# Query projections of a cross attention and five gate panels in seven block products

## The chip, the cores and the metric

One core of a Trainium2 chip runs the whole program. The time is that of one execution on the device in microseconds (us). Everything is computed in fp32.

## The reference

Two transformer blocks follow each other on 256 rows of width 1024. The parts that the change touches, with their shapes:

```
# first block: token mixer, once
proj  = h @ w_in                       # [256, 1024] @ [1024, 7880]
gates = proj[:, 4808:]                 # 3 x 1024 columns: a, b, c
score = sum_h w_idx[h] * relu(q_idx[h] @ k_idx.T / 8) / sqrt(8)   # 8 index heads
keys  = the 64 largest scores of each row                         # for attention c
y = sigmoid(gates_a) * (o_a @ w_branch_a) + sigmoid(gates_b) * (o_b @ w_branch_b)
  + sigmoid(gates_c) * (o_c @ w_branch_c)

# second block: cross attention on a memory of 256 rows, in each of 2 layers
q    = (x @ wq).reshape(256, 4, 256)   # wq [1024, 1024]
k, v = split(memn @ wkv)
x    = layer_norm(alpha * x + softmax(q @ k.T / 16) @ v @ wo)
```

## The kernel before

TensorE (PE) multiplies, VectorE (DVE) adds, combines and normalizes, ScalarE (ACT) copies results out of PSUM and computes exponentials and sigmoids, GpSimd (POOL) makes one sum per panel and clears paddings, and SyncE (SP) issues the loads of the weights. Each engine has its order written out by hand, in one block of the program each; semaphores that only count upwards tie them together. There is no scheduler.

**Panels.** The weights pass as panels of 1024 x 512 values (2 MB) through a ring of four slots. SP issues the load of panel n when panel n - 4 has counted up `panel_done`. `P_WIN + j` are the panels of the first block's input projection: nine whole ones, one of 200 columns, then six gate panels, of which the sixth (the late gate) is multiplied in eight pieces between the units of the first attention. `L_WQ`, `L_WQ + 1` are the two panels of the query projection in a layer.

**Seven products.** The two feed-forward networks, the nine whole panels of the first input projection and three of each layer's split activations and weight panel into 2 x 2 blocks and form the result from seven products of blocks in place of eight. That costs sums. DVE makes three sums of weight quarters per panel (`weight_sums`, lines 1886 to 1890, each 128 x 1024 values; it counts up `forms_ready`), the fourth sum is POOL's (`fourth_sums`, line 610, `fourth_ready`) or DVE's own (line 1893). `act_sums` (lines 1902 to 1907) makes the sums of the turned activations once, when both tiles have been turned. ACT copies the first product out of its bank (`first_out`), and DVE combines the rest in three to four additions (lines 1934 to 1941 where rows of the result lie on the partitions, 2400 to 2412 where its columns do). `project` (product on line 822) works in rows and `expand_turned` (line 878) in columns. Both start with the first tile: turn it, products 1 and 2 of panel 0 (a head), turn the second tile, head of panel 1, then products 6, 7, 5, 4, 3 (a tail) of each. Product 6 waits for `forms_ready`, product 4 for `fourth_ready`.

**Eight products.** The gate panels (`gate` on PE, line 1127) are multiplied plainly, 16 matmuls with 512 columns each, in two halves, one for each tile of 128 rows; ACT's sigmoid reads the banks directly (line 1540). Between the halves PE turns the heads of the three attentions (`batch`, line 977, in banks 4 and 5) and computes index scores (`index_scores`, line 1160). ACT applies the relu to them (line 1555), DVE adds them up with their weights (line 2188) and, after four of them, takes the 64 largest of a tile in eight rounds of eight (lines 2202, 2204). The query projection of a layer (`weight_stationary`, line 716) is 32 matmuls with 256 columns per panel; ACT copies and scales the result (line 1671). Ahead of it PE multiplies half of the memory's values (`memory_values(1, ...)`, line 1351, copied out by ACT on line 1694) and turns both tiles of the normalized rows (batches `E_X1`).

**The first attention** (`attend`) runs 20 units. In step j PE computes the scores of unit j, turns the weights of unit j - 2 and multiplies values of unit j - 3; DVE makes the logits (line 2030) and, in the first eight units, mixes two maps (line 2057). The last four units need the selected keys.

## Time and profile before

| what | us |
|---|---|
| median of 3 runs | 1814.26 |
| lowest, highest | 1813.68, 1817.46 |
| the profiled execution, whole | 1820.03 |
| its span from first to last instruction | 1818.2 |
| PE busy in it | 1751.6 |
| DVE busy | 1058.7 |
| ACT busy | 360.0 |
| POOL busy | 191.0 |
| mean granted clock of TensorE | 0.99 of 2.4 GHz |

All durations used below are of the profiled execution. A line of a timeline merges neighbouring records of one form: its start, the time from its start to its end, and the idle time of the engine before it with what ended that. The starts of neighbouring lines give the pace; the ends of matmuls are modelled and reach a little over the next start.

### The profile page before, as it was taken

Reading aid. Unit: us, or ns where it says so; the run is one execution under the profiler, and the core shown is the slowest. Engines: PE = TensorE matmul, PEld = TensorE weight load, DVE = VectorE, ACT = ScalarE, POOL = GpSimd, SP = SyncE. Lnnn points to the kernel's source line nnn. Section 1 sums busy time; section 2 is a strip of 40 time slices with the busy share of each in tenths; the row PEclk is TensorE's granted clock in tenths of the full one; section 3 lists DMA queues with packets and bytes.
Section 4 is the critical chain, followed back from the end, with each engine's and each line's share of the span. In section 5 each row is a group of like instructions: output and inputs, shape, how many; then the busy total and the mean of one; then the engine's idle time right before and its main releaser. Section 6 shows DMA issues by size and latency. Waiting matters only on the chain.

```text
span 1818.2 us, 22081 instructions
## 1 busy us (share of the span) xinstructions
PE 1751.6 (96%) x8510; PEld 1293.5 (71%) x8510; DVE 1058.7 (58%) x2084; ACT 360.0 (20%) x884; POOL 191.0 (11%) x126
## 2 busy tenths in 40 slices
PE   6999999999999999999999999999999999999997
PEld 5887478744747885476784859984668766689953
DVE  5776468724654786641172158995712541479985
ACT  1111000033411110102271212220012530222210
POOL 1221211100011122120001000002110000000020
PEclk9999999999899999999999999999999999999999
DMA  9643454531166454436314335443455205165440
GB/s 313 207 154 142 159 185 157 185 116 70 55 209 202 148 183 162 147 105 192 139 45 142 124 116 180 150 180 131 143 145 190 88 1 208 47 209 167 159 162 23
DMA packets 162502, 265.59 MB, mean 146 GB/s; under 512 B 4008, under 2 KB 105684, under 8 KB 162270
## 3 DMA queue, kind: packets, MB, share of 16 engines
q1 hardware_dynamic: 157470, 248.18, 40.2%
q0 software_dynamic: 4768, 15.48, 2.5%
q8 instruction: 68, 1.11, 0.3%
q10 hardware_dynamic: 160, 0.52, 0.1%
q14 instruction: 36, 0.29, 0.1%
HBM read 262.56 MB, written 1.08 MB: 145 GB/s over the span
## 4 chain that ended last, share of the span: by engine, by line
PE 76%; DVE 14%; DVEq 4%; ACT 3%; issue 2%; DMA 1%; SPq 1%; ACTq 0%
PE psum L766 15%; PE psum L926 11%; PE psum L822 10%; PE psum L739 8%; PE psum L1044 4%; PE psum L1127 3%; PE psum L1079 3%; PE psum L1308 3%; PE psum L1351 3%; PE psum L716 3%; DVE work L2379 3%; PE psum L977 2%; DVE ring L1888 2%; PE psum L729 2%; PE psum L965 2%
## 5 line engine op out<-in xcount | busy, mean ns | idle before, releaser
L610 POOL TENSOR_TENSOR work<-ring,work 128x1024 f32<-128x1024 f32 (+1 forms) x57 | 141.5, 2483 | 808.9 <-DVE work L1890 808.9
L926 PE MATMUL psum<-ring,work 128*128 128x512 f32 x352 | 162.2, 596 | 3.5 <-DVE work L2412 3.5
L1886 DVE TENSOR_TENSOR work<-ring 128x1024 f32<-128x1024 f32 (+1 forms) x83 | 100.8, 1214 | 84.9 <-PE psum L926 80.8
L739 PE MATMUL psum<-ring,x_t 128*128 128x512 f32 x320 | 140.0, 595 | 7.4 <-ACT x_t L1408 7.4
L926 PEld LDWEIGHTS psum<-ring,work 128*128 128x128 f32 x352 | 66.5, 190 | 85.3 <-issue 80.1
L926 PE MATMUL psum<-work 128*128 128x512 f32 x264 | 123.1, 595 | 0.0
L739 PEld LDWEIGHTS psum<-ring,x_t 128*128 128x128 f32 x320 | 60.0, 190 | 81.5 <-issue 71.8
L1888 DVE TENSOR_TENSOR ring<-ring 128x1024 f32<-128x1024 f32 (+1 forms) x83 | 102.3, 1233 | 6.2
L1890 DVE TENSOR_TENSOR work<-ring 128x1024 f32<-128x1024 f32 (+1 forms) x83 | 99.6, 1200 | 6.2
L926 PEld LDWEIGHTS psum<-work 128*128 128x128 f32 x264 | 50.1, 192 | 62.9 <-issue 61.2
L2030 DVE CUSTOM_DVE_ANT_0 work<-psum,work 128x256 f32<-128x256 f32 (+1 forms) x96 | 31.4, 365 | 108.8 <-PE psum L1044 108.7
L1044 PE MATMUL psum<-work 128*128 128x256 f32 (+2 forms) x416 | 85.3, 337 | 3.4 <-ACT work L1671 2.2
L766 PE MATMUL psum<-ring,x_t 128*128 128x256 f32 x352 | 83.2, 391 | 3.7 <-ACT x_t L1408 2.2
L878 PE MATMUL psum<-x_t,work 128*128 128x128 f32 x704 | 85.8, 275 | 0.0
L878 PE MATMUL psum<-work,ring 128*128 128x128 f32 x704 | 85.8, 275 | 0.0
L2379 DVE SCALAR_TENSOR_TENSOR work<-work 128x254 f32<-128x254 f32 (+1 forms) x176 | 83.5, 527 | 3.3
L878 PE MATMUL psum<-x_t,ring 128*128 128x128 f32 x704 | 82.6, 276 | 2.8 <-ACT x_t L1408 2.8
L1408 ACT ACTIVATE work<-psum 128x512 f32<-128x512 f32 (+4 forms) x84 | 44.9, 562 | 194.5 <-PE psum L977 163.0
L766 PE MATMUL psum<-work,x_t 128*128 128x256 f32 x352 | 83.2, 379 | 0.0
L766 PE MATMUL psum<-ring,work 128*128 128x256 f32 x352 | 83.2, 379 | 0.0
L878 PEld LDWEIGHTS psum<-x_t,ring 128*128 128x128 f32 x704 | 80.4, 192 | 3.8 <-ACT x_t L1408 3.8
L878 PEld LDWEIGHTS psum<-x_t,work 128*128 128x128 f32 x704 | 82.1, 192 | 0.0
(258 smaller groups left out, 2919.9 us busy)
## 6 DMA issues: line engine op xcount, KB each, us to landing
ring<-in_ffn_w_up_dram SPq DMA_DIRECT2D x66, 1024.0 KB, 7.9
ring<-in_w_in_dram SPq DMA_DIRECT2D x21, 2048.0 KB, 7.8
ring<-in_ffn_w_down_dram SPq DMA_DIRECT2D x20, 2048.0 KB, 7.7
ring<-in_ffn_w_gate_dram SPq DMA_DIRECT2D x22, 1024.0 KB, 5.4
ring<-in_xa_wkv_dram SPq DMA_DIRECT2D x8, 2048.0 KB, 7.9
ring<-in_w_out_dram SPq DMA_DIRECT2D x6, 2048.0 KB, 8.7
ring<-in_xa_wq_dram SPq DMA_DIRECT2D x4, 2048.0 KB, 7.8
ring<-in_xa_wo_dram SPq DMA_DIRECT2D x4, 2048.0 KB, 9.4
```

The source lines that it names most:

```text
L610: nc.gpsimd.tensor_tensor(t4, quarters(n, chunks, pitch)[2], t2, ALU.subtract).then_inc(fourth_ready, 1)
L716: last = mm(o[:, c * T:(c + 1) * T], ring[:, n % RING, k * 512 + c * P:k * 512 + (c + 1) * P], acts[:, k, :], start=(k == 0), stop=(k == K ...
L739: return mm(bank(banks[2 * i + h]), acts[:, c, i * P:(i + 1) * P], ring[:, (n0 + c // 4) % RING, o:o + 512], start=(c == 0), stop=(c == KD ...
L766: last = mm(corners(j)[p], acts[p][:, i, :], rhs[:, i, :], start=(i == 0), stop=(i == KD // 2 - 1))
L822: last = mm(row_corners(j)[p], acts[p][:, i, :], rhs[:, i, :], start=(i == 0), stop=(i == KD // 2 - 1))
L878: last = mm(corners(j)[p][:, c * P:(c + 1) * P], weights[:, i, c * P:(c + 1) * P], acts[p][:, i, :], start=(i == 0), stop=(i == KD // 2 - 1))
L926: last = mm(sums[p], acts[p][:, q, :], rhs[:, i, :], start=(q == 0), stop=(q == KF // 2 - 1))
L1044: last = mm(PS[:, o:o + x["keys"]], q, k[:, 0:x["keys"]], start=(c == 0), stop=(c == len(pairs) - 1))
L1886: v.tensor_tensor(t3, b22, b12, ALU.subtract)
L1888: v.tensor_tensor(b12, b12, b11, ALU.subtract)
L1890: v.tensor_tensor(t2, b22, b12, ALU.subtract).then_inc(forms_ready, 1)
L2379: last = v.scalar_tensor_tensor(dst, UP[:, q, 0:T - t], CWT[:, 2 - t, k:k + 1], dst, ALU.mult, ALU.add)
```

## The change

Five of the six gate panels are computed by seven products in rows, with the items that stood between the halves now dealt out between the products. Their weight sums lie in places that are free at that time: the sums of gate 0 where gates 1 and 2 will lie, those of gate 1 in the place of the turned queries, those of gates 3 and 4 in ring slots of earlier panels. POOL writes the fourth sum in place over the block of product 2, so it waits for product 6. SP therefore waits for gate panel 3 before it loads the sixth, and for panel 4 before the branch weights. The sums of gates 0 and 1 are made in the last two steps of the projection before. The order of the gates becomes a, a, c, c, b, b; the sigmoid is applied to the combined rows in SBUF, and for both halves of b only after the attention. DVE deals out index sums and selection rounds between the steps of the combination, and four rounds of the second tile go to steps 8 to 11 of the first attention.

The query projection of each layer goes through `expand_turned` with two panels. It starts when the first tile is turned, in banks that no longer include those of the memory values (now 6 and 7); the output projection before it moves to banks 0 to 3. The factor 1/16 of the queries is applied to the copy of the keys.

```diff
-GATE_ORDER = (0, 1, 2, 4, 5, 3)
+GATE_ORDER = (0, 1, 4, 5, 2, 3)
+GATES = 5
-FOURTH_ON_VECTOR = [F_UP1, F_UP1 + 1, F_UP2, F_UP2 + 1] + [F_LUP + F_LAYER * l + j for l in range(LAYERS) for j in range(UPS)]
+FOURTH_ON_VECTOR = [F_UP1, F_UP1 + 1, F_UP2, F_UP2 + 1] + [F_LQ + F_LAYER * l + j for l in range(LAYERS) for j in range(LQS + UPS)]
...
         def sums_of_weights(f, chunks, pitch):
 
+            if F_GATE <= f < F_GATE + GATES:
+                q = f - F_GATE
+                n = P_WIN + 8 + q
+                v = (w(W_GATES + D, 2, KD // 2, 256), w(W_QTA, 2, KD // 2, 256), w(W_GATES + 3 * D, 2, KD // 2, 256),
+                     ring[:, n % RING, 0:2 * D].rearrange("p (t i c) -> p t i c", t=2, i=KD // 2),
+                     ring[:, n % RING, 0:2 * D].rearrange("p (t i c) -> p t i c", t=2, i=KD // 2))[q]
+                return [v[:, 0], v[:, 1], quarters(FORM_PANELS[f], chunks, pitch)[2]]
...
                 n = P_WIN + 10 + j
+                if j == 5:
+                    sp.wait_ge(panel_done, P_WIN + 14)
                 load(n, [(slot(n, KD, 512), win[:, :, C_GATE + 512 * GATE_ORDER[j]:C_GATE + 512 * GATE_ORDER[j] + 512])])
+            sp.wait_ge(panel_done, P_WIN + 15)
...
                     pool.wait_ge(forms_ready, f + 1)
+                    if F_GATE <= f < F_GATE + GATES:
+                        pool.wait_ge(part_done, 2 * (C_SIDE + f - F_GATE) + 1)
...
+            def gate_panel(q, relus, between):
+
+                arrived(P_WIN + 10 + q)
+                group(G_WIN + 10 + q)
+                if relus:
+                    pe.wait_ge(relu_ready, relus)
+                pe.wait_ge(first_out, C_SIDE + q)
+                gate_product(q, 1).then_inc(first_done, 1)
+                gate_product(q, 2)
+                for item in between.get(2, ()):
+                    item()
+                pe.wait_ge(forms_ready, F_GATE + q + 1)
+                gate_product(q, 6).then_inc(part_done, 1)
...
+                pe.wait_ge(fourth_ready, F_GATE + q + 1)
+                gate_product(q, 4)
...
+                gate_product(q, 3).then_inc(panel_done, 1)
...
+            gate_panel(0, 0, {6: [turn_index(0)], 7: [turn_index(1)], 5: [turn_index(2)]})
+            gate_panel(1, 0, {6: [index_scores(0, 1)], 7: [index_scores(1, 1)], 5: [index_scores(2, 1)], 4: [index_scores(3, 1)]})
+            gate_panel(2, 4, {2: [turn_a(0)], 6: [index_scores(4, 2), turn_a(1)], 7: [turn_a(2)],
+                              5: [index_scores(5, 2), turn_a(3)], 4: [turn_a(4)]})
+            gate_panel(3, 6, {2: [turn_a(5)], 6: [index_scores(6, 3), turn_b(0)], 7: [turn_b(1)],
+                              5: [index_scores(7, 3), turn_b(2)], 4: [turn_b(3)]})
+            gate_panel(4, 8, {2: [turn_c(0)], 7: [turn_c(1)]})
...
-                residual_product(L_OUT, XT, (2, 3, 4, 5), turn_mixed(E_O, U1 + TT + 12, 19, l), l)
-
-                memory_values(1, (0, 1), (0, 1))
-                turn_rows(E_X1, X, 21, l, 11)
-                pe.wait_ge(turned_out, at(E_X1 + 4, B_LAYER, l))
-                for j in range(2):
-                    weight_stationary(L_WQ + j, H_WQ + j, XT, l)
+                residual_product(L_OUT, XT, (0, 1, 2, 3), turn_mixed(E_O, U1 + TT + 12, 19, l), l)
+
+                memory_values(1, (0, 1), (6, 7))
+                expand_turned(L_WQ, LQS, F_LQ + F_LAYER * l, H_WQ, C_LQ + C_LAYER * l, A_LQ + A_LAYER * l, turn_tile_of(E_X1, X, 21, 11, l), l)
                 pe.wait_ge(group_free, at(H_WQ + 2, G_LAYER, l))
...
+            gate_combined(0)
+            gate_combined(1, after_fifth=first_two_sums)
+            index_sum(2)
+            index_sum(3)
+            masked_scores(0)
...
+            gate_combined(2, lambda: take_eights(0, 2), fifth_sum)
+            index_sum(5)
+            gate_combined(3, lambda: take_eights(0, 2), last_of_first_tile)
+            index_sum(7)
+            masked_scores(1)
+            gate_combined(4, lambda: take_eights(1, 2), lambda: take_eights(1, 2))
...
+            attend(UNITS_1, 0, None, {**{j: lambda: take_eights(1, 1) for j in (8, 9, 10)}, 11: take_last})
...
                 attend(UNITS_2, U1, l)
                 both_tiles()
-                layer_norm(15, gains_in(4, l), l, residual(L_OUT + 1, 2, (2, 3, 4, 5), 1.0, ALPHA, l))
+                f0, c0 = F_LQ + F_LAYER * l, C_LQ + C_LAYER * l
+                weight_sums(f0, KD, 512)
+                layer_norm(15, gains_in(4, l), l, residual(L_OUT + 1, 2, (0, 1, 2, 3), 1.0, ALPHA, l))
+                dve.wait_ge(turned_out, at(E_X1 + 4, B_LAYER, l))
+                mid, last = act_sums(XT, XS[0:3], 0)
...
+                weight_sums(f0 + 1, KD, 512)
+                for j in range(LQS):
+                    combine_fourths = up_combined(j, c0, XQT[:, 4 * j:4 * j + 4, :])
+                    dve.wait_ge(panel_done, FORM_PANELS[f0 + j] + 1)
+                    combine_fourths()
```

## Rows read from the trace of the kernel before

**Rows 1.** The page, part 1 (PE) and part 4: busy time, and the chain by engine.

```profile
PE 1751.6 (96%) x8510; PEld 1293.5 (71%) x8510; DVE 1058.7 (58%) x2084; ACT 360.0 (20%) x884; POOL 191.0 (11%) x126
...
PE 76%; DVE 14%; DVEq 4%; ACT 3%; issue 2%; DMA 1%; SPq 1%; ACTq 0%
```

**Rows 2.** Windows, gate stage: length, busy us of each engine, clock, DMA, GB/s.

```profile
351.70:435.00 83.30, 81.85 (x250) 38.43 (x249) 22.44 (x79) 25.01 (x57) 4.01 (x7) 1.00 0.30 109
```

**Rows 3.** Timeline of PE, query projections of the first layer.

```profile
996.15 1.91 PE L977 MATMUL psum<-ident_flip,x_res 128*128 128x128 f32 x16
999.45 27.89 PE L716 MATMUL psum<-x_t,ring 128*128 128x256 f32 x128 [1.39 <-ACT x_t L1408]
1028.46 1.78 PE L1044 MATMUL psum<-work 128*128 128x256 f32 x7 [1.11 <-ACT work L1671]
```

**Rows 4.** Timeline of PE, gate stage: start, us, engine, line, operation, count [idle before].

```profile
351.74 7.03 PE L1127 MATMUL psum<-ring,x_t 128*128 128x512 f32 x16
...
368.01 0.70 PE L1160 MATMUL psum<-work 64*128 64x256 f32 x4
...
368.64 7.13 PE L1127 MATMUL psum<-ring,x_t 128*128 128x512 f32 x16
...
375.61 1.04 PE L977 MATMUL psum<-ident_flip,work 128*128 128x128 f32 x8
...
435.02 0.68 PE L1044 MATMUL psum<-work 128*128 128x128 f32 x4 [1.22 <-issue]
```

**Rows 5.** Timeline of PE, second feed-forward of the first block: two products of a panel.

```profile
593.22 1.89 PE L766 MATMUL psum<-work,x_t 128*128 128x256 f32 x8
594.95 1.89 PE L766 MATMUL psum<-ring,work 128*128 128x256 f32 x8
```

**Rows 6.** Timeline of PE, feed-forward expansion of the first layer, its first two panels.

```profile
1077.13 3.84 PE L878 MATMUL psum<-x_t,ring 128*128 128x128 f32 x32 [0.74 <-ACT x_t L1408]
...
1102.52 1.95 PE L878 MATMUL psum<-work,ring 128*128 128x128 f32 x16
...
1104.31 3.74 PE L878 MATMUL psum<-x_t,ring 128*128 128x128 f32 x32
```

**Rows 7.** Timeline of DVE, panels of the first block's input projection.

```profile
321.97 0.68 DVE L1934 TENSOR_TENSOR work<-work,psum 128x512 f32<-128x512 f32 x1
...
327.02 1.23 DVE L1890 TENSOR_TENSOR work<-ring 128x1024 f32<-128x1024 f32 x1
...
328.33 3.41 DVE L2120 TENSOR_TENSOR work<-work 128x1024 f32<-128x1024 f32 x1
...
333.12 1.23 DVE L2120 TENSOR_TENSOR work<-work 128x1024 f32<-128x1024 f32 x1
```

**Rows 8.** Timeline of POOL, the same stretch.

```profile
328.32 2.35 POOL L610 TENSOR_TENSOR work<-ring,work 128x1024 f32<-128x1024 f32 x1 [3.83 <-DVE work L1890]
```

**Rows 9.** Timeline of DVE, end of the selection: one round to the next.

```profile
435.79 0.43 DVE L2202 MAX8 work<-work 128x8 f32<-128x256 f32 x1
...
436.85 0.43 DVE L2202 MAX8 work<-work 128x8 f32<-128x256 f32 x1
```

**Rows 10.** Timeline of PE, first attention: its two waits for DVE.

```profile
441.28 0.33 PE L1061 MATMUL psum<-ident_flip,work 128*128 128x128 f32 x1 [1.25 <-DVE work L2057]
...
460.78 0.44 PE L1061 MATMUL psum<-ident_flip,work 128*128 128x128 f32 x2 [0.85 <-DVE work L2057]
```

**Rows 11.** Timeline of ACT, before the query projections of the first layer.

```profile
997.31 2.08 ACT L1408 ACTIVATE x_t<-psum 128x512 f32<-128x512 f32 x4
```

**Rows 12.** The page, part 6: a weight panel, KB, median us from issue to landing.

```profile
ring<-in_w_in_dram SPq DMA_DIRECT2D x21, 2048.0 KB, 7.8
```

**Rows 13.** Windows of PE behind the first attention: length, busy, granted clock, DMA, GB/s.

```profile
487.50:490.00 2.50, 2.50 (x15) 0.55 0.00 0
...
495.00:497.50 2.50, 2.50 (x4) 0.50 0.00 0
```

**Rows 14.** The page, part 5: a weight load of this form, count, busy, mean ns.

```profile
L878 PEld LDWEIGHTS psum<-x_t,work 128*128 128x128 f32 x704 | 82.1, 192 | 0.0
```

More of the change, by code:

```diff
@@ L1198, in _, with turn_c, turn @@
[L1198 to L1203 removed]
+                return lambda: turn_heads(B_B + c, heads_b[2 * c:2 * c + 2])
+            def turn_c(c):
+                def turn():
+                    pe.wait_ge(heads_ready, 4)
+                    turn_heads(B_C + c, [P1[:, :, C_CQ + j * P:C_CQ + (j + 1) * P] for j in range(2)] if c == 0 else [dup[:, 1, :, :]])
+                return turn
@@ L1547, in late_gate_out, with index_relu @@
                 for i in range(TT):
-                    last = copy(late[:, i, :], bank(1 + 2 * i))
+                    last = copy(gates[5][:, i, :], bank(1 + 2 * i))
                 last.then_inc(group_free, 1)
-            def index_relu(u):
+            def index_relu(u, q):
                 act.wait_ge(raw_ready, u + 1)
@@ L1622, in _ @@
             batch_out(B_O + 3, XT[:, 4:6, :])
-            activation(late, late, ACT.Sigmoid).then_inc(late_gate, 1)
+            act.wait_ge(group_free, G_WIN + 15)
+            late = w(W_GATES + 4 * D, 2, TT, 512)
+            for i in range(TT):
+                activation(late[:, :, i, :], late[:, :, i, :], ACT.Sigmoid).then_inc(late_gate, 1)
             nc.scalar.preload_act_table_set(logs_and_exps)
@@ L1995, in bias_of, with attend @@
                 return zero_bias[:, 0:x["keys"]]
-            def attend(units, u0, l=None):
+            def attend(units, u0, l=None, between={}):
                 def logits(j):
@@ L2198, in _, with keys_of, masked_scores, take_eights @@
+            def keys_of(i):
+                return SEL[:, i, 0:P * (i + 1)]
+            def masked_scores(i):
+                n, o = P * (i + 1), P * (1 - i)
+                v.tensor_scalar(masked[:, 0:n], TB[:, 12, o:o + n], NEG / 2, NEG, ALU.is_lt, ALU.mult)
                 dr()
-                v.tensor_tensor(work, score[:, 0:n], m, ALU.add)
+                v.tensor_tensor(keys_of(i), score[:, 0:n], masked[:, 0:n], ALU.add)
                 dr()
-                for _ in range(NSEL // 8):
-                    v.max(top8, work)
+            def take_eights(i, rounds):
+                for _ in range(rounds):
+                    v.max(top8, keys_of(i))
```

403 lines of the change are left out of this document (216 added, 187 removed).

## The prediction

> **What bounds the kernel now.** I read the page's engine totals first, then the chain that ended last: TensorE (PE) is busy for 1751.6 of the 1818.2 us of the span, and the chain runs over it for 76% [rows 1]. So the question is what PE has to do and for whom it waits, stage by stage. The windows of the gate stage come next: in its 83.3 us PE is busy for 81.85, VectorE (DVE) for 22.44 and ScalarE (ACT) for 25.01 [rows 2]. There DVE and ACT have room, and PE work taken away should shorten the stage by itself. The cross attention's projections look the same: one uninterrupted piece of 27.89 us on PE, with a wait on either side [rows 3].
>
> In the trace an fp32 matmul leaves two records, so a gate panel of 16 matmuls is 32 records, and a seven-product panel of 28 matmuls with half the columns is 56.
>
> **1. Five gate panels, products alone.** Before, half a panel after index scores takes 375.61 - 368.64 = 6.97 us [rows 4]; ten halves are 69.7. After, each product is 4 matmuls of 256 columns, 8 records; where the kernel runs this form already, one follows another after 594.95 - 593.22 = 1.73 us [rows 5]. 5 x 7 x 1.73 = 60.55. Gain 9.15.
>
> **2. What stands between the products.** The eight pairs of index scores (0.63 us each [rows 4]) and the 56 transposes of heads remain, but are dealt out singly: some seven more changes between kinds of work. No row prices one. It is at least nothing, and at most 0.3 us: two whole turns of a tile, copies included, add 27.18 - 14 x 1.79 = 2.1 in [rows 6], for four batches and two waits. I take 0.1 each, nearer to nothing, since the trace shows no PE idle at such a change: +0.7.
>
> **3. Waits of PE inside the gate stage.** I walked the four queues through the stage with the durations above. Before each product 6 PE waits for the weight sums of its panel. Those three DVE operations and the three to four that combine the previous panel take 328.25 - 321.97 = 6.3 us together, where 328.25 is the end of the last sum [rows 7]. The sums of panels 0 and 1 are made in the last two panels of the projection before, the others two panels ahead, some 20 us early: hidden. If that cover went, each would cost up to 3.8 us (three operations of 1.23 and their gaps). The fourth sum is POOL's, 2.35 us [rows 8]; it may begin only after product 6 of its own panel and is needed after products 7 and 5, at least 3.46 us later, so about 1.1 is spare. What queues behind it on POOL are the memsets of the paddings; the attention waits for the last, which comes a panel earlier than that. I find four short waits that do appear: panel 0 makes PE wait for the copies of the index keys, since DVE has 7.7 us of weight sums more ahead of them (0.5 left); the fourth index score waits for ACT, which has the first sigmoid and its table in front and needs DVE's first sum out of its two buffers (0.6); two batches wait for ACT's copies of a batch of keys (0.2 each). Together +1.5, with bounds of 0.3 and 7 (a block of 2.2 us as in part 6, three times).
>
> **4. The end of the stage.** Before, PE waited 1.22 us for the last sigmoid to empty its banks [rows 4]. Now the scores' first banks were last used by panel 3, which is combined while panel 4 runs, and the scores need no more than that: -1.22. DVE made all eight selection rounds of the second tile after the last index sum, 1.06 us each [rows 9], and therefore came late to the first logits: PE's wait of 1.25 [rows 10]. Four rounds now lie inside panel 4 and four between units 8 to 11 of the attention: -1.25. There DVE has little room, as PE's wait of 0.85 for the same operation shows [rows 10]; of 4 x 1.06 = 4.2 us of added work the idle gaps of DVE and PE's lead over it absorb most, and I take +0.8 (bounds 0 and 4.2).
>
> **5. Query projections, two layers.** Before: from the first transpose at 996.15 to the first score at 1028.46, 32.31 us [rows 3]. After, PE may start when the first tile is turned: ACT copies the memory values, then two of its four batches, 997.31 + 2.08 / 2 = 998.35 [rows 11], so head 0 starts near 998.4. From there it is exactly what the expansion does in its first two panels, heads, second turn and both tails: 1104.31 - 1077.13 = 27.18 [rows 6]. That ends at 1025.6. DVE's last combination costs between 0.68 (the operation alone [rows 7]) and the 1.11 that ACT's copy cost [rows 3]; 0.9 gives 1026.5. Gain 1.95 a layer. I count 1.9, or 3.8 for both; bounds 1.2 and 2.6. DVE gets 4.9 us of sums ahead of the layer norm and as much behind it; the first lies beside 14 us of output projection, the second beside head 1 and tail 0 (12.6 us) as in the expansion. The scale of the queries goes onto the keys' copy and costs nothing. The product form itself earns little: 14 x 1.79 = 25.1 for 27.9.
>
> The Trainium skill speaks against this part. Its page "TensorE: Matmul & The Clock Gate", section "Back-to-back issue gap", gives some 81 ns as the sustained spacing of matmuls with 128 columns because weight loads count too, and 56 ns as the isolated one. The rows have 16 records in 1.79 us, 112 ns or twice 56, so here they go with the isolated figure. By the sustained one a product would be 16 x 0.162 = 2.6 us and the 28 products of both layers 22.7 us more, an estimate from that page: 1824.5 in all.
>
> **6. Queues passed.** SP issues the sixth gate's load only after panel 3, and the three branch loads after panel 4, because sums lie in those slots. The sixth gate is needed after one more panel (12.1 us at least) plus the first scores, and a panel lands 7.8 us after issue [rows 12]; cover left about 4. The branch loads have the whole attention as cover. DVE and POOL collide: a DVE operation of two SBUF operands that takes 1.23 us took 3.41 while POOL's fourth sum of 2.35 us ran [rows 7, 8]. So each fourth sum can hold DVE for 2.2 us. In the gate stage DVE's next operations then are index sums; ACT's buffers and with them PE's next score wait behind those. My walk has 1 us or more in hand at each.
>
> The page "SBUF — State Buffer" of the Trainium skill, section "Who interferes with whom", says that a DVE instruction with two SBUF inputs and a GpSimd one that reads SBUF block each other fully, and whoever issues first wins; the row agrees. By that rule DVE may win too, and then a fourth sum comes late. This is rival B.
>
> **Sum.** -9.15 + 0.7 + 1.5 - 1.22 - 1.25 + 0.8 - 3.8 = -12.4. The profiled execution took 1820.03 us (span 1818.2), so after 1807.6; the median of the runs shown is 5.8 lower, 1814.26, and gives **1801.8**.
>
> **Rivals.**
> A, the forecast: 0.66.
> B, waits take a good part of it back. Every gate panel now hangs on two DVE sums, POOL's fourth sum and ACT's first copy, where it hung on nothing but the weights. For it: the collision above, and 1.1 us of slack on POOL. Against: DVE busy for 22.4 of 83.3. Price: three panels late by 2.2 are 6.6: 1808. Chance 0.14.
> C, TensorE's clock. Behind the first attention it fell to half: four windows of 2.5 us at 0.50 to 0.55, PE busy for 8.5 of them, some 4.2 us lost [rows 13]. What comes ahead is small matmuls with waits between. The new stage has more and shorter pieces. One more such fall gives 1806 (0.04). If the clock stays up behind the attention because DVE is punctual, 1797.6 (0.08).
> D, the other side: gate stage, both layers and attention each give the clock a reason to fall. Only from four falls of 4.2 us on, 16.8, is all spent: 1818.6. Against it: PE's new waits are under 1 us each, and the 1.39 in front of the projections [rows 3] was followed by records at the full pace. 0.02.
> E, again the other side: seven products with 128 columns pay for their weight loads. A load takes 0.19 us [rows 14], longer than the 0.112 from one matmul record to the next. Were the loads not hidden, the 28 products of both layers, 448 records, would cost 35 us more: 1836.8. 0.02, since 22 panels of this form run at 0.112 in this trace.
> F, the change doesn't do what it says in time: the shorter products are there, but DVE, with the heads' norms, index sums, selection and combinations in one queue, becomes the bound of the gate stage. DVE's load rises by five combinations (2.5 each), three weight sums (3.8) and some 8 us pushed in from before, less 4.2 of selection: 22.4 + 28 = 50 of 75 us. It would have to be stopped for 25 more. 1812: 0.04.
>
> **Numbers.** Range 1796.5 to 1808.5: from one fall of the clock less and the better bound of part 5, to B's price. Faster by over 0.2% (3.6 us, about what a measurement of this kernel can tell from none): A, B, most of C and a part of F, 0.91; within 0.2%: 0.05; slower: 0.04.
>
> **What would show it.** Gate stage: 35 products 1.73 apart, the first attention scores 74 to 76 us behind the first gate product instead of 83.3; PE's waits inside it under 1 us each. The first transpose in the attention without the 1.25, and up to 1 us more waiting around units 8 to 12. Cross attention: head 0 some 2.2 us behind the first transpose, scores at 30.4. Half clock behind the first attention as before. I am wrong if a fourth or weight sum ends late and PE waits for POOL or DVE for over 1 us in several panels, if the products are further apart than 1.73 and 1.79, or if a window of half clock stands where none stood.

## Result, and the profile after the change

The changed kernel took 1796.03 us in the median of four executions (1794.09 to 1799.33). The kernel before took 1815.86 us beside it, so the ratio is 0.9884, with an interval of [0.9872, 0.9897]. The forecast was 1801.8 us with a range from 1796.5, so the measured median lies just below it. The profiled execution took 1795.17 us, with a span of 1793.4.

With twelve more of the later runs there are sixteen executions of the changed kernel: their median is 1801.5 us (1794.09 to 1808.60). The later runs also hold 66 executions of the kernel before, with a median of 1816.5 (1807.88 to 1820.76). Each of the two kernels spreads over 13 to 15 us by itself, and that spread is what the result turns on.

The page of after, part 1 and the chain by engine, answers to [rows 1]:

```profile
PE 1727.9 (96%) x8822; PEld 1309.5 (73%) x8822; DVE 1127.3 (63%) x2159; ACT 358.8 (20%) x884; POOL 202.9 (11%) x131
...
PE 76%; DVE 15%; DVEq 4%; ACT 2%; issue 2%; DMA 1%; SPq 1%; ACTq 0%
```

PE is busy for 23.7 us less than in [rows 1] and bounds the kernel as before. Not all of that is work taken away: a second profile of the kernel before, without the half clock of the first (experiment 1), has PE busy for 1741.1 us, so at nearly equal clock the changed kernel saves 13.2. The windows of the gate stage answer to [rows 2] (length, busy us of PE, weight loads, DVE, ACT, POOL, then clock, DMA, GB/s):

```profile
349.60:423.20 73.60, 73.28 (x369) 60.15 (x368) 51.08 (x115) 27.61 (x56) 17.54 (x13) 1.00 0.26 95
```

DVE went from 22.44 to 51.08 us, and PE is still busy for all but 0.3 us. The timeline of PE, panel 1 of that stage, answers to [rows 4]; L1147 is `gate_product`, L1209 an index score:

```profile
366.19 1.89 PE L1147 MATMUL psum<-work 128*128 128x256 f32 x8
368.01 0.70 PE L1209 MATMUL psum<-work 64*128 64x256 f32 x4
368.64 1.99 PE L1147 MATMUL psum<-work 128*128 128x256 f32 x8
...
376.07 0.70 PE L1209 MATMUL psum<-work 64*128 64x256 f32 x4 [0.32 <-ACT work L1589]
376.70 1.99 PE L1147 MATMUL psum<-ring,work 128*128 128x256 f32 x8
378.54 3.62 PE L1147 MATMUL psum<-ring,x_t 128*128 128x256 f32 x16
```

A product follows another after 1.73 us (two of them from 378.54 to 381.99), with 0.1 more for each index score next to it: 1.82 from 366.19 to 368.01, 1.93 from 368.64 to 370.57. Transposes cost it nothing: the second product of panel 0, with transposes behind it, takes 1.72 (353.01 to 354.73). The only wait in the whole stage is the 0.32. The first layer's query projection answers to [rows 3]; L898 is the product in columns:

```profile
978.88 1.04 PE L997 MATMUL psum<-ident_flip,x_res 128*128 128x128 f32 x8
981.20 3.84 PE L898 MATMUL psum<-x_t,ring 128*128 128x128 f32 x32 [1.28 <-ACT x_t L1444]
984.88 1.04 PE L997 MATMUL psum<-ident_flip,x_res 128*128 128x128 f32 x8
986.65 3.84 PE L898 MATMUL psum<-x_t,ring 128*128 128x128 f32 x32 [0.74 <-ACT x_t L1444]
...
1006.41 1.95 PE L898 MATMUL psum<-work,ring 128*128 128x128 f32 x16
1009.23 3.04 PE L1064 MATMUL psum<-work 128*128 128x256 f32 x13 [0.87 <-DVE work L2473]
```

From the first transpose to the scores it is 30.35 us, where it was 32.31.

**Where the time went, stage by stage.** The table sets marks of PE against each other, in four executions. It is worked out from the starts in the timelines; what differs between two executions of the same kernel is almost all clock. Left out are the stretch from the output projection to the first transpose of the queries, 43.18 us in each column and layer, and what follows the queries of layer 1.

| stretch | before | before, again | after | after, third |
|---|---|---|---|---|
| start to first gate product | 351.74 | 349.68 | 349.55 | 351.45 |
| gate stage | 83.28 | 83.28 | 73.68 | 73.68 |
| attention, to the branch product | 58.93 | 56.85 | 57.17 | 59.95 |
| branches | 32.22 | 30.22 | 30.22 | 32.99 |
| output and feed-forward | 242.36 | 242.35 | 242.71 | 242.72 |
| layer 0, to its output projection | 184.44 | 182.44 | 182.37 | 184.65 |
| layer 0, queries | 32.31 | 32.31 | 30.35 | 30.35 |
| layer 0, scores to layer 1 | 262.36 | 260.61 | 259.92 | 259.87 |
| layer 1, to its output projection | 184.26 | 182.55 | 182.64 | 184.73 |
| layer 1, queries | 32.30 | 32.31 | 30.35 | 30.34 |
| span | 1818.2 | 1806.5 | 1793.4 | 1806.8 |

Read across, the structure is: gate stage -9.60, attention +0.32, the stretch behind the branches +0.36, queries -1.96 and -1.96, together -12.8. The prediction's sum was -12.4. The spans of the two first profiles differ by 24.8, and the rest is of the size of the difference between the first and the second column, or the third and the fourth: 11.7 us between two executions of one unchanged kernel, 13.4 between two of the other. Not clock, and not of the change either, are some tenths ahead of the gates and one wait of PE for DVE at the end of a layer's feed-forward: it is 2.06 us in layer 0 of before_again and 1.33 in layer 1, in the changed kernel's first profile 1.39 and 2.10. Hence 260.61 against 259.92. What makes it long in one layer or the other isn't shown.

### The profile page after: what moved, and what is told of

Same layout as the page of the kernel before. It is cut to its first block, busy times and chain, and to the rows that moved or that the text cites. A ratio compares the mean times of both kernels' runs of the same rounds, so it can differ in the third digit from the quotient of the medians.

```text
span 1793.4 us, 22877 instructions
## 1 busy us (share of the span) xinstructions
PE 1727.9 (96%) x8822; PEld 1309.5 (73%) x8822; DVE 1127.3 (63%) x2159; ACT 358.8 (20%) x884; POOL 202.9 (11%) x131
## 4 chain that ended last, share of the span: by engine, by line
PE 76%; DVE 15%; DVEq 4%; ACT 2%; issue 2%; DMA 1%; SPq 1%; ACTq 0%
PE psum L786 15%; PE psum L946 12%; PE psum L842 10%; PE psum L759 8%; PE psum L898 5%; PE psum L1064 3%; PE psum L1147 3%; PE psum L1347 3%; PE psum L1390 3%; PE psum L1099 3%; DVE work L2509 3%; PE psum L997 2%; DVE ring L1941 2%; PE psum L749 2%; PE psum L884 2%
## 5 line engine op out<-in xcount | busy, mean ns | idle before, releaser
L1939 DVE TENSOR_TENSOR work<-ring 128x1024 f32<-128x1024 f32 (+1 forms) x90 | 110.8, 1232 | 80.3 <-PE psum L946 77.6
L1941 DVE TENSOR_TENSOR ring<-ring 128x1024 f32<-128x1024 f32 (+1 forms) x92 | 113.3, 1232 | 6.8
L1943 DVE TENSOR_TENSOR work<-ring 128x1024 f32<-128x1024 f32 (+1 forms) x90 | 108.2, 1202 | 6.7
L898 PE MATMUL psum<-x_t,ring 128*128 128x128 f32 x832 | 98.0, 276 | 6.9 <-ACT x_t L1444 6.9
L898 PE MATMUL psum<-x_t,work 128*128 128x128 f32 x832 | 101.4, 275 | 0.0
L898 PE MATMUL psum<-work,ring 128*128 128x128 f32 x832 | 101.4, 275 | 0.0
L898 PEld LDWEIGHTS psum<-x_t,ring 128*128 128x128 f32 x832 | 94.9, 192 | 8.8 <-ACT x_t L1444 8.8
L898 PEld LDWEIGHTS psum<-x_t,work 128*128 128x128 f32 x832 | 97.1, 192 | 0.0
L898 PEld LDWEIGHTS psum<-work,ring 128*128 128x128 f32 x832 | 97.1, 192 | 0.0
```

Source lines behind the costliest of these rows:

```text
L898: last = mm(corners(j)[p][:, c * P:(c + 1) * P], weights[:, i, c * P:(c + 1) * P], acts[p][:, i, :], start=(i == 0), stop=(i == KD // 2 - 1))
L1939: v.tensor_tensor(t3, b22, b12, ALU.subtract)
L1941: v.tensor_tensor(b12, b12, b11, ALU.subtract)
L1943: v.tensor_tensor(t2, b22, b12, ALU.subtract).then_inc(forms_ready, 1)
```

## Experiments

**1. The kernel before, once more.**

> The unchanged kernel once more, to see how its granted clock and its stretches at half clock differ from one execution to the next. Theory 1 (the falls of the clock come and go with the execution, and the profiled execution of before had many by chance): a profile of it shows some other number of falls than the seven of the first profile, at other places, and times that move with it by up to 6 us. Theory 2 (they are fixed by what the kernel does at those places): the same places, near 22, 487, 852, 910, 1228, 1375 and 1432 us, and a mean clock of 0.990 again. Ratio 1.000 in both.

Its profiled execution had a span of 1806.5 us where the first had 1818.2. Windows of all engines where the attention ends, the stretch of [rows 13], here 2.1 us earlier in the execution:

```profile
485.00:487.50 2.50, 2.16 (x20) 1.97 (x18) 0.86 (x5) 0.69 (x2) 0.00 (x0) 1.00 0.00 0
487.50:490.00 2.50, 1.29 (x9) 1.05 (x10) 2.33 (x4) 1.08 (x2) 0.00 (x0) 1.00 0.02 7
```

The clock is 1.00, although PE waits there exactly as before, 1.38 us for ACT and 0.81 for DVE. Windows over the whole trace show no half clock but the one at the end of the program, where the first profile has seven stretches besides that (at 22, 487, 852, 910, 1227, 1375 and 1432 us). Theory 1 holds. The profile that the prediction was read from held one execution with many falls, and [rows 13] is not there in every execution. It isn't rare either: of the fifteen kept profiles of all kernels here, eight have half clock behind the first attention.

**2. The gates alone.** The query projection is as before (`weight_stationary`), the gates are as changed.

```diff
-WINS, LWINS, LQS = 9, 3, 2
+WINS, LWINS, LQS = 9, 3, 0
...
-                expand_turned(L_WQ, LQS, F_LQ + F_LAYER * l, H_WQ, C_LQ + C_LAYER * l, A_LQ + A_LAYER * l, turn_tile_of(E_X1, X, 21, 11, l), l)
+                turn_rows(E_X1, X, 21, l, 11)
+                pe.wait_ge(turned_out, at(E_X1 + 4, B_LAYER, l))
+                for j in range(2):
+                    weight_stationary(L_WQ + j, H_WQ + j, XT, l)
```

> The gate panels in seven products alone; the query projections are as before. By the rows of the two traces the gate stage takes 73.7 us in place of 83.3, and the attention behind it is 0.3 longer where the clock is full in both: 9.3 us, 1806.5. Theory 1 (the rest of the gain is the clock, by chance of the execution): 1802 to 1809 and no fixed clock. Theory 2 (the gates' change itself keeps the clock up): 1800 and below, mean clock 0.995 or more in every execution. Theory 3 (the gain beyond the sum comes from the query projections' change): 1806 with the clock of before, 0.990.

1807.09 us (1803.48 to 1809.42), ratio 0.995. Gate stage 73.69, attention 57.12, queries 32.31. Against the kernel before at the same mean clock, its four executions stand 9.4, 11.0, 9.3 and 8.4 below (at 0.990, 0.991, 0.992 and 0.995), 9.5 in the mean, where 9.3 was expected from the stages. The clock was anywhere from 0.990 to 0.995: theory 1 holds, and theory 2, with 0.995 or more in every execution, does not. The stretch behind the branches is 242.71 here and 242.35 in the next kernel, so the 0.36 belongs to the gates.

**3. The query projections alone.** The gates are as before.

```diff
-GATES = 5
...
+            gate(0, 0)
+            pe.wait_ge(heads_ready, 3)
+            turn_heads(B_IDX, [P1[:, :, C_IQ + j * P:C_IQ + (j + 1) * P] for j in range(4)] + [dup[:, :, 0, :]])
+            gate(0, 1)
...
```

> The query projections in seven products alone; the gates are as before. By rows: 2.0 us less in each layer, 4.0 together, 1811.8. Theory 1: 1808 to 1814, clock anywhere between 0.990 and 0.997. Theory 2 (gates hold the clock): 1811.8 at a clock of 0.990. Theory 3 (this part does): 1806 or below, at 0.995 or more.

1813.23 us (1809.42 to 1814.64), ratio 0.9979. Queries 30.34 and 30.35, gate stage 83.28: the two parts add up and do not touch each other. Clocks of 0.990 to 0.994 rule out theory 3; theories 1 and 2 can't be told apart by them.

**4. No selection in the attention.** All eight rounds of the second tile lie ahead of the first logits.

```diff
+            take_eights(1, 3)
+            take_eights(1, 1)
+            selected(1)
-            attend(UNITS_1, 0, None, {**{j: lambda: take_eights(1, 1) for j in (8, 9, 10)}, 11: take_last})
+            attend(UNITS_1, 0)
```

> The changed kernel with all eight selection rounds of the second tile ahead of the first attention, instead of four of them in its steps 8 to 11. If the dealing out is worth what the prediction said: VectorE is 4.2 us later at the first logits, PE waits 1 to 3 us at the first transpose of the attention, and not the 1.4 us at units 8 and 9: between 0.5 us faster and 3 us slower than the changed kernel. If the start's wait was what made the clock fall behind the first attention, half clock stands there again and it is 4 to 6 us slower.

1805.66 us (1804.57 to 1808.31). Timeline of PE, start of the attention:

```profile
428.73 0.71 PE L1064 MATMUL psum<-work 128*128 128x128 f32 x4 [1.81 <-DVE stat L2092]
430.87 0.33 PE L1081 MATMUL psum<-ident_flip,work 128*128 128x128 f32 x1 [1.42 <-DVE work L2116]
```

```profile
430.00:432.50 2.50, 1.63 (x3) 0.72 1.02 415
432.50:435.00 2.50, 2.50 (x9) 0.59 0.84 336
```

PE waits 3.2 us for DVE in two pieces, and the second block (windows of PE: length, busy, clock, DMA, GB/s) shows half clock behind them, which no other profile has there. With the 0.85 at unit 8 its waits for DVE are 4.1 us. The changed kernel has three waits in their place, 1.9 together with one of 0.26 for ACT (shown under part 4 below), so spreading the rounds is worth some 2.2. Half clock stands behind the attention too (from 479 us). The start's waits are not its cause: the same stretch falls in experiments 5 and 6, where they are absent.

**5 and 6. The changed kernel, twice more.**

> The changed kernel once more, unaltered, to see how its granted clock spreads over more executions. The kernel before had mean clocks of 0.990 to 0.998 over 29 executions (1807.9 to 1818.9 us), the changed kernel 0.994 to 0.997 over four (1794.1 to 1799.3). Theory T1 (the number of half clock stretches is a matter of the single execution, and four executions fell well by chance): ten more executions spread over 0.990 to 0.998, their median clock lies near 0.992 as before, and the median time near 1801 to 1803 us, since the structural gain is 13 us on 1815. Theory T2 (the changed kernel by itself keeps the clock up more often, since TensorE no longer meets the two waits ahead of the first attention): at least eight of ten executions at 0.994 or above, median time 1795 to 1798 us, ratio to the kernel before 0.988 to 0.990. In both, where TensorE's clock is full the stages last as in the first profile: gates 73.7, query projections 30.35 us.

Six executions: 1801.03, 1802.80, 1804.65, 1802.70, 1795.37, 1802.01; mean clocks 0.994, 0.993, 0.990, 0.993, 0.998, 0.993. T1 was right on the median (1802.36).

> The changed kernel a third time, unaltered. So far its mean clock was 0.9945 over ten executions (0.990 to 0.998), that of the kernel before 0.9924 over 54; at equal clock the changed one is 12.8 to 14 us quicker. Theory T1 (how often the clock falls is the same in both, ten executions were lucky): mean clock 0.992 to 0.993 in the new executions, median 1802 to 1804 us. Theory T2 (the changed kernel keeps the clock up more often): again 0.994 or more, median 1796 to 1801 us.

Six more: 1808.60, 1802.70, 1794.89, 1800.87, 1806.92, 1804.82; mean clocks 0.987 to 0.998, mean 0.9913. T2 falls. Behind the attention, after and after_third do the same work; windows of PE in the one and in the other:

```profile
475.00:477.50 2.50, 2.21 (x20) 1.00 0.00 0
477.50:480.00 2.50, 1.34 (x11) 1.00 0.03 7
480.00:482.50 2.50, 2.10 (x5) 1.00 0.01 3
```

```profile
475.00:477.50 2.50, 1.11 (x10) 0.91 0.00 0
477.50:480.00 2.50, 2.50 (x14) 0.50 0.00 0
480.00:482.50 2.50, 1.69 (x9) 0.50 0.00 0
...
487.50:490.00 2.50, 2.50 (x4) 0.50 0.15 54
```

Both wait 1.38 or 1.39 us for ACT in or just ahead of the first of these windows. In the third execution the clock then stays at 0.50 into the branch product, whose first 24 records take 13.34 us in place of 10.57. Besides the end of the program, the profile of after has one stretch of half clock (1410), after_again two (475, 1727) and after_third eight (22, 475, 760, 845, 902, 1277, 1362, 1735).

Sorted by the mean clock of the execution, in the means of all executions:

| mean clock | before | after | difference |
|---|---|---|---|
| 0.990 | 1818.78 (9) | 1804.74 (2) | -14.0 |
| 0.993 | 1815.17 (11) | 1802.55 (4) | -12.6 |
| 0.994 | 1813.89 (10) | 1800.18 (2) | -13.7 |
| 0.998 | 1808.16 (3) | 1795.13 (2) | -13.0 |

The mean clock doesn't fix the time to the microsecond: the nine executions of the kernel before at 0.990 lie between 1817.38 and 1820.05.

**7. Both tiles turned first.** The second turn no longer stands between the heads. The four batches of transposes also get a PSUM bank each, where two shared one; what that alone does isn't told apart.

```diff
                 turn_tile(0)
+                if together:
+                    turn_tile(1)
                 head(0)
-                turn_tile(1)
+                if not together:
+                    turn_tile(1)
                 head(1)
```

> The changed kernel with one difference: in the query projections both tiles of the rows are turned ahead of head 0, not the second between the heads, and act_sums is made at once. This prices the interleaving that the change took over from the expansion. Theory I (the second turn between the heads costs TensorE its copies and changes, nothing else): 3.8 us of turning, a wait of up to 1 us for the last copies, 14 products of 1.79 (25.1), and 0.8 for the last combination, so turn to scores 30.0 to 30.7, as now within 0.4 us. Theory S (only one wait is left, since the sums of activations come earlier): 29.3 us, 1 us a layer less, 2 us in all. Theory W (head 0 must wait for all four copies as it did before, 1.4 us, and product 6 for the sums of activations, over 1 us): 31.5 us or more, a loss of 1 us a layer.

1800.05 us (1795.71 to 1803.89), ratio 0.9911. Timeline of PE:

```profile
979.19 1.91 PE L1000 MATMUL psum<-ident_flip,x_res 128*128 128x128 f32 x16
982.49 7.41 PE L898 MATMUL psum<-x_t,ring 128*128 128x128 f32 x64 [1.39 <-ACT x_t L1448]
```

29.45 us from turn to scores, 0.9 less a layer, close to theory S. One wait of 1.39 takes the place of 1.28 and 0.74. In this stage, starting with the first tile does not pay for itself, since head 0 waits for ACT in either order.

**8. The turning hidden behind the memory's values.** As experiment 7, with ACT's copies of the turned rows ahead of those of the values, and:

```diff
-                memory_values(1, (0, 1), (6, 7))
+                memory_values(1, (0,), (6, 7))
+                turn_rows(E_X1, X, 21, l, 11)
+                memory_values(1, (1,), (6, 7))
```

> As the run with both tiles turned first, and the turning lies between the two tiles of the memory's values, so that ACT's copies of the turned rows run beside 7 us of the second tile's product. From the end of the output projection to the first scores of the cross attention it is now 73.53 us, in the kernel before 75.49. If the wait for the copies is all that stands between (theory I and S alike), it is 14 products of 25.1, values 14 x 2 and turning 3.8 with no wait: 71.0 to 71.6, 2 us a layer less, 4 us in all: at the same clock 1791 to 1793. If product 6 then waits for act_sums or the first sums of weights, because DVE's layer norm ends only ahead of the turning, over 72.5 us.

Timeline of PE:

```profile
972.61 1.91 PE L1000 MATMUL psum<-ident_flip,x_res 128*128 128x128 f32 x16
974.36 7.03 PE L1393 MATMUL psum<-ring,work 128*128 128x512 f32 x16
981.23 7.31 PE L898 MATMUL psum<-x_t,ring 128*128 128x128 f32 x64
```

The copies run beside the product on L1393 and no wait is left. From the start of the output projection to the scores it is 36.31 + 34.66 = 70.97 us, in place of 73.53 (the expectation says "end", but its 73.53 is counted from the start). Median 1793.82 us, ratio 0.9878.

**9. Weight sums one panel ahead.** This takes away the cover named in part 3 of the prediction.

```diff
-                if q + 2 < GATES:
-                    weight_sums(F_GATE + q + 2, KD, 512)
+                if 2 <= q + 1 < GATES:
+                    weight_sums(F_GATE + q + 1, KD, 512)
```

> The changed kernel with the weight sums of gates 2 to 4 made one panel ahead in place of two, after the combination of the panel just before: this takes away the cover of which the forecast said that without it each sum costs up to 3.8 us. Theory A (the cover is what keeps TensorE from waiting, DVE is close behind): product 6 of panels 2, 3 and 4 waits 0.7 to 1.2 us each, the gate stage is 75.8 to 77.2 us in place of 73.7. Rival F (DVE is nearly the bound of the stage): over 4 us a panel, stage over 82. Rival N (DVE has room anyway and one panel ahead suffices): no wait over 0.3 us, stage 73.7 to 74.2.

1804.75 us (1802.66 to 1809.47), ratio 0.9935. Timeline of PE, its waits for DVE in the gate stage:

```profile
383.67 1.99 PE L1147 MATMUL psum<-work 128*128 128x256 f32 x8 [0.62 <-DVE work L1943]
400.53 1.99 PE L1147 MATMUL psum<-ring,work 128*128 128x256 f32 x8 [0.62 <-DVE ring L1943]
417.39 3.72 PE L1147 MATMUL psum<-ring,work 128*128 128x256 f32 x16 [0.62 <-DVE ring L1943]
```

The stage takes 76.35 us, 2.67 more or 0.89 a panel. Theory A holds for the stage (75.8 to 77.2), with waits a little under its 0.7 to 1.2: 1.86 us of the 2.67 stand in the three waits, the rest in steps where the view shows none. DVE misses product 6 by under 1 us with one panel of lead, and two panels are what hides it.

**10. The fourth sum two products later.** Rival B, brought about.

```diff
-                        pool.wait_ge(part_done, 2 * (C_SIDE + f - F_GATE) + 1)
+                        pool.wait_ge(part_done, 2 * (C_SIDE + f - F_GATE) + 2)
```

> The changed kernel, but GpSimd may begin the fourth sum of a gate panel only behind product 5, not product 6: two products (3.46 us) and what stands between them later. This makes rival B of the forecast happen on purpose and prices it. Theory A (the fourth sum costs GpSimd 2.35 us and hands over in some 0.1, and had 1.1 to 1.6 us in hand): TensorE waits at product 4 for 2.4 us less what stands between 5 and 4, that is 2.4, 1.7, 1.3, 1.3 and 2.4 in the five panels, about 9 us; gate stage 82.3 to 83.3 us in place of 73.68. Rival B in full (GpSimd's sum, now beside index sums of VectorE with two operands in SBUF, also holds those for up to 2.2 us a panel, and TensorE's next scores behind them): over 86 us. Rival N (the sum is not on TensorE's path): under 76 us.

1816.10 us (1810.97 to 1819.84), ratio 0.9995: the gain of the whole change is gone. PE's waits, in three of the five panels:

```profile
364.37 2.97 PE L1147 MATMUL psum<-ring,x_t 128*128 128x256 f32 x8 [2.33 <-POOL ring L631]
382.63 1.99 PE L1147 MATMUL psum<-ring,x_t 128*128 128x256 f32 x8 [1.92 <-POOL ring L631]
...
433.93 3.46 PE L1147 MATMUL psum<-ring,x_t 128*128 128x256 f32 x8 [2.55 <-POOL ring L631]
```

With 1.34 in each of the other two they are 9.5 us, and about 9 was expected of theory A. But the stage took 86.81 us, 13.1 more, which is the band named for rival B in full. The cause is another one. Most of the rest is the clock, in windows of PE:

```profile
362.50:365.00 2.50, 0.63 (x3) 1.00 0.00 0
365.00:367.50 2.50, 2.50 (x8) 0.55 0.03 7
...
432.50:435.00 2.50, 1.07 (x3) 0.70 0.00 0
435.00:437.50 2.50, 2.50 (x9) 0.62 0.00 0
```

Both are at the two longest waits, 2.33 and 2.55; at the three of 1.34 to 1.92 it stayed up. Products 4 and 3 of these two panels take 2.76 + 2.48 and 3.29 + 1.73 us where they take 1.73 each: 3.3 us together; 0.3 stays unexplained. The collision is there too, in DVE and POOL of this kernel, and then DVE of after at the same operation:

```profile
380.22 2.36 POOL L631 TENSOR_TENSOR ring<-ring,work 128x1024 f32<-128x1024 f32 x1 [15.90 <-PE psum L1147]
381.21 1.52 DVE L2247 TENSOR_SCALAR work<-work 128x256 f32<-128x256 f32 x1
```

```profile
374.33 0.35 DVE L2247 TENSOR_SCALAR work<-work 128x256 f32<-128x256 f32 x1
```

The first index sum was held from 0.35 to 1.52 us while POOL's sum took no longer than alone. It cost PE nothing that the timeline shows. The unaltered changed kernel has such a collision as well, in timelines of its DVE and POOL:

```profile
374.75 1.62 DVE L2249 SCALAR_TENSOR_TENSOR work<-work 128x256 f32<-128x256 f32 x3
383.08 4.12 DVE L2249 SCALAR_TENSOR_TENSOR work<-work 128x256 f32<-128x256 f32 x4
384.47 2.45 POOL L631 TENSOR_TENSOR ring<-ring,work 128x1024 f32<-128x1024 f32 x1 [3.65 <-PE psum L1147]
```

Four index sums, 0.54 us each elsewhere, took 4.12, about 2 us more, and PE did not wait for them.

**11 and 12. Selection rounds two steps later, twice.**

```diff
-            attend(UNITS_1, 0, None, {**{j: lambda: take_eights(1, 1) for j in (8, 9, 10)}, 11: take_last})
+            attend(UNITS_1, 0, None, {**{j: lambda: take_eights(1, 1) for j in (10, 11, 12)}, 13: take_last})
```

> The changed kernel with the four selection rounds of the second tile at steps 10 to 13 of the first attention in place of 8 to 11. From the first score to the branch product, at full clock, the attention takes 56.85 us in the kernel before and 57.17 in the changed one, with waits for VectorE of 1.40 where unit 8 follows unit 7, and of 0.26 and 0.22 right behind. Theory L (the rounds at steps 8 and 9 hold VectorE where it is late anyway, while it idles 0.4 to 0.8 us a step further on): the wait goes back to 0.85, the two behind it vanish, 55.7 to 56.2 us, so 1.0 to 1.5 us less; with the forecast's own sum (-1.25 for the first wait, no added cost) it would be 55.6. Rival M (VectorE has no room at steps 12 and 13 either, where logits of 0.95 us follow each other): 57.0 us or more, the waits move to units 12 to 15.

> The changed kernel with the selection rounds at steps 10 to 13 once more. Its four executions had clocks of 0.988 to 0.992, lower than the changed kernel's, though the stage that differs is 0.6 us shorter at full clock (56.53 us, read from the kernel with both edits). Theory T1 (chance): mean clock 0.992 to 0.993, the same as the changed kernel beside it within 0.001, median 1801 to 1803. Theory K (each kernel has its own habit of falling, set by where its instructions and waits lie): again 0.991 or less, 1804 to 1806 us.

The medians are 1805.47 and 1802.31 us, with mean clocks of 0.990 and 0.9916. Over the nine executions the clock is 0.9909, below the changed kernel's 0.9933 over sixteen, whose own three groups have 0.996, 0.9935 and 0.9913. The second group's median fits theory T1, the first group's does not, and whether theory K is true can't be said from this. The stage itself is read at full clock from experiment 13: 56.53 in place of 57.17 us, 0.6 less, where theory L expected 1.0 to 1.5 less and rival M 57.0 or more: neither is met. The wait of 1.40 went back to 0.85 and the two behind it went, but a new one of 0.27 appears.

**13. Both improvements.** Experiment 8 with the rounds of experiment 11.

> The version that the runs point to: the changed kernel with both tiles turned between the memory's values (71.0 us from the end of the output projection to the cross attention's scores, 73.53 in the changed kernel) and the selection rounds at steps 10 to 13. If both gains add up: 2 x 2.55 + 1.3 = 6.4 us below the changed kernel at equal clock, that is 1789.0 us at a mean clock of 0.998, 1796 at 0.993, median 1793 to 1797 over several executions. Against it: if the rounds at steps 12 and 13 only move the wait, 1.3 less of that gain.

1795.31 us in the median of five (1789.95 to 1799.28), ratio 0.9874 [0.9854, 0.9895]. It took 1799.28 at a mean clock of 0.990, 1796.77 at 0.992 and 1789.95 and 1791.65 at 0.996, where the changed kernel took 1804.74, 1800.87 and 1796.88. It is thus 5.5, 4.1 and 6.1 us quicker at the same clock, by few executions, where the stages say 2 x 2.56 + 0.64 = 5.8.

## Why the prediction was right in most of its steps and missed the number

**The step that failed is the clock.** The prediction took the falls of its one profile as given, looked at those behind the attention only [rows 13], and priced a change of them as rival C with single falls. Two things were wrong in it. First, the profile held six more stretches; the gate stage has full clock [rows 2], timelines don't show the clock, and the mean of 0.99 in the table of before was passed over. Second, their number is not the kernel's: it runs from none to seven in two profiles of the kernel before, and from one to eight in three of the changed one. 0.001 of mean clock is worth 1.2 us (4.9 us from 0.990 to 0.994 in the table above). So a median of few executions moves by several us with no cause in the code, and the range of +7 and -5 us around the forecast had no term for that. The first four executions of the changed kernel had clocks of 0.994 to 0.997, a mean of 0.996; the twelve that followed had 0.992 and a median of 1802.7, inside the range. By the 1.2 us, those 0.0036 of clock are 4.4 of the 6.7 us between the two medians; the rest has no cause on record. The median over all sixteen, 1801.5 us, is 0.3 from the forecast, but that too owes something to chance: the difference at equal clock is about 13 us and the forecast stands 12.4 below a median of 1814.26 that later runs put at 1816.5.

Of the rivals, C with the clock up behind the attention (1797.6) names the time nearest to the measured one. Its reason does not hold: DVE is just as punctual in after_again and after_third, and the clock falls there.

The sum itself, -12.4 against -12.8 measured in the stages, hides errors that cancel. The gate stage was taken at -8.2 (with the last sigmoid) and gave -9.6; the attention at -0.45 and gave +0.32; the 0.36 behind the branches was not in it.

**Part 1, products.** Taken at 1.73 us each, and they are where no index score is next to them. The rule of the Trainium skill that the prediction weighed ("TensorE: Matmul & The Clock Gate", "Back-to-back issue gap") would have put the 28 products with 128 columns further apart. The trace of after has 1.79 us for 16 records, 112 ns each, in the query projections as in the expansion. That is again twice the isolated 56 ns, and rival E is out.

**Parts 2 and 3, changes and waits.** 10.37 us were to be gained by the products and the last sigmoid, and 9.60 came: 0.77 lost, where the prediction took 0.7 + 1.5. Of the four waits only that of the fourth index score is there, 0.32 for 0.6; the copies of the index keys and the two batches made PE wait for nothing that the trace shows. The 0.7 for "some seven more changes" was miscounted: PE goes from one kind of work to another 25 times in the stage of before and 43 times in that of after, 18 more. The other 0.45 us is less than the 0.7 all the same, because only index scores cost anything, about 0.1 us on each side, and transposes nothing that the starts show; the 6.97 taken for each half of before already held one such side. The 1.22 before the first scores has "issue" as its end in [rows 4]; that it was the last sigmoid is read from the code, and it is gone. That the sums are hidden with two panels of lead is shown by experiment 9; without it they cost 0.9 a panel, well below the upper bound of 3.8.

**Part 4, the attention.** -1.25 + 0.8 was taken, +0.32 measured, the one term with a wrong sign. The first transpose has no wait, as said. The added selection was mis-sized: it cost 1.6 us, not 0.8. Timeline of PE in after, which answers to [rows 10]:

```profile
448.34 0.44 PE L1081 MATMUL psum<-ident_flip,work 128*128 128x128 f32 x2 [1.40 <-DVE work L2116]
451.61 0.52 PE L1081 MATMUL psum<-ident_flip,work 128*128 128x128 f32 x3 [0.26 <-ACT work L1537]
452.97 1.53 PE L1064 MATMUL psum<-work 128*128 128x256 f32 x6 [0.22 <-DVE stat L2092]
```

The wait of 0.85 grew to 1.40, two short ones follow, and some 0.5 lies in steps where the view shows no wait. The prediction counted on the lead of PE and DVE's idle gaps; at step 8, where the mixing of unit 7 is still in DVE's queue, there is neither. Two steps later 0.6 of it is saved.

**Part 5, queries.** 1.9 a layer was taken, 1.96 measured. Head 0 starts 2.32 us behind the first transpose (2.2 said), and the last combination costs 1.03 (0.9 said): from the last product at 1006.41 to the scores is 2.82, less 1.79. That the product form earns little by itself is right, but the prediction did not see that the other order is better still: the late turn costs 0.9 a layer, and hiding the turn saves 1.7 more.

**Part 6 and rival B, the queues.** No wait for POOL, and no collision that PE feels: POOL's fourth sums take 2.35 to 2.63 us in the gate stage, and the 2 us that one of them cost DVE (experiment 10) reach nobody. Experiment 10 also shows what a late sum would do. The page "SBUF — State Buffer" of the Trainium skill ("Who interferes with whom") has the two engines block each other, and whoever issues first wins. The index sum that came 1 us after POOL's was the one held. Rival B's price was put at 6.6 us for three late panels. With five panels late it is 9.5 us of waits and 3.3 of clock, so a wait of over 2 us on PE can cost more than its own length.

**Rivals D and F.** DVE is busy for 51 of 73.7 us (50 of 75 were reckoned), and does not bound the stage. Four falls and more do occur, in after_third, but none of its eight lies in the gate stage or the query projections, and five, that at the end of the attention among them, lie where the kernel before falls as well.

**What stays open.** The 0.36 us behind the branches is a wait for DVE ahead of layer 0 that grew from 0.83 to 1.18; its cause was not looked for. What decides whether the clock falls at one of its places in a given execution isn't shown by any run here. The places return from kernel to kernel: behind the first attention, at the start of a layer, and 84 and 142 us into it. The wait behind the first attention was not filled or removed to see whether the clock then stays up.

## What to carry to other kernels

Before a forecast of under 1%, look through the clock of the whole trace, forecast the stages at full clock, and give the range a term for half clock from the spread of several executions; set two kernels against each other by stages at full clock or by executions of equal mean clock. In block products protect the sums' lead in panels, and let the engine with the late sum start at least that sum's length before it is needed. Put new work for a busy engine where that engine idles, even if it is a step later, not where it is already late.

## What the runs showed of the hardware

The same instructions behind the same wait of 1.38 us were followed by full clock in some executions (before_again, after) and by 10 to 14 us at half clock in others (before, after_again, after_third). Waits of 2.33 and 2.55 us in the gate stage were each followed by half clock, those of 1.34 to 1.92 us in the same execution were not. How much a stretch costs depends on what runs in it: those behind the attention cost 4.1 us in the kernel before (2.08 in the attention and 2.00 in the branches) and 5.5 in after_third, while the one at 1410 us of after cost 0.15 (182.64 us, against 182.49 for the same stretch of layer 1 in after_again, which has none there). DVE operations on SBUF that began while POOL's sum of 2.35 to 2.45 us ran took longer than elsewhere: 1.52 us for 0.35 (experiment 10), about 2 us more for one of four index sums in after, 3.41 for 1.23 in the kernel before [rows 7, 8].
